# Spreading two gate rows over the partitions by DMA, and one value burst per group of the windowed attention

## The chip, the core and the metric

The kernel runs on one core of a Trainium2 chip. The metric is the device time of one execution in microseconds (us). The engines are TensorE (PE, whose weight loads are listed apart as PEld), VectorE (DVE), ScalarE (ACT), GpSimd (POOL) and SyncE (SP). SP issues nearly all DMAs; a few come from ACT's own queue. About 0.2% of the time (3.1 us) is what a measurement of this kernel can tell from no change.

## The reference

Two equal layers of a trunk are computed for five token tiles of 128 (four tiles of latent tokens, numbered 0 to 3, and one tile of context tokens, called LT). In each layer, cut to what matters here:

```python
def modulate_project(x, mod, w_in):
    shift, scale, gate = jnp.split(mod, 3, axis=-1)
    u = (layer_norm(x) * (1.0 + scale) + shift).astype(x.dtype)
    return split_columns(u @ w_in), gate

def attend_band(q, k, v, kc, vc, sink):      # branch C, |i - j| <= 128, plus 128 cached context keys
    ...
    p = softmax_with_sink(jnp.concatenate([s_band, s_ctx], axis=-1), sink).astype(v.dtype)
    o = (jnp.einsum('bkgnqs,bknsd->bkgnqd', p[..., :nband], vband)
         + jnp.einsum('bkgnqs,bksd->bkgnqd', p[..., nband:], vc))

def merge_residual(x, ys, zs, g_merge, gate, w_branch, w_out, ln_g, ln_b, alpha):
    gates = jnp.split(jax.nn.sigmoid(g_merge), N_BRANCH, axis=-1)
    merged = sum(gb * ((yb * jax.nn.silu(zb)) @ w_branch[i])
                 for i, (yb, zb, gb) in enumerate(zip(ys, zs, gates)))
    h = alpha * x + gate * (merged @ w_out)
    return (layer_norm(h) * ln_g + ln_b).astype(x.dtype)
```

`mod = silu(c) @ w_mod + b_mod`. Its last third, `gate`, is one row of 1024 numbers for the latent tokens and another for the context tokens. These two rows are the output gates of the title: every token of a tile is multiplied by the same row.

## The kernel before

Each layer is a list of weight pieces of 512 KB (two blocks of 128 rows by 512 columns). SP loads each piece into one of the three buffers of `raw`. For the projections GpSimd (in places ACT) splits it into a rounded part and a remainder in `wsp` or a slot, and TensorE multiplies with three products per block, 30 matmuls for a piece over five token tiles (L1057, by `product`). The order is written out by hand, engine by engine. PSUM has eight banks; `PsumPlan` says ahead which result uses which bank after which, and the engines wait for each other through `bank_full` and `bank_done`.

A layer runs branch A (attention), C (windowed attention) and B (mLSTM), in this order, and then the output projection. Branch C of layer 0 has a loop of 43 steps, of which the first 32 each handle one unit, that is one head for one latent tile. Step s does, on TensorE: the scores of unit s (L1252), the transposes of unit s - 3's probabilities (L1277), one part of a late modulation (`late_step`: L1001 products straight from a `raw` piece of `w_mod`, every fourth time the bias, L1008, and in a later step a transpose of the row, L1033) and then `values` for v = s - 8 (L1326). Four units are a group: two heads of one key head times two tiles. The value products of group g were made in two bursts: at v = 4g (part 0) those for the cached context keys and the first key block, at v = 4g + 2 (part 2) those for the other two blocks. Both read `pT`, the transposed probabilities of all four units, which part 0 waits for. The groups are eight; group g has its part 0 at step 4g + 8.

The late modulation of layer 0 needs 24 pieces of `w_mod`, used at steps 1, 4 and 7 to 28. A piece is not split; SP loads the piece three places on as soon as `mod_used` says that TensorE is through with the buffer. Chunk n of the modulation ends as one row per quarter of 128 columns, and DVE copies it to `mrow` (L2053). The last two chunks of a layer are the output gates. At that point the rows that matter are partitions 0, 32, 64 and 96 of `mrow` for the latent tokens and 1, 33, 65 and 97 for the context tokens, 128 numbers each, for both halves of `mrow`.

After the loop comes the merge projection G of branch C, half 0. It has four pieces, i = 0 to 3. Behind piece 2, `gates` (L1145) multiplied a column of the identity, repeated 128 times, with `mrow`: 16 fp32 matmuls per layer, which copy each row to all partitions of four PSUM banks. ACT copied the four banks to `gate_bc` (L1850), 128 partitions by 1024 for both kinds of tokens. ACT then takes the tanh of each G tile (L1938), and DVE uses the tanh and the branch product BR, whose banks are those of the G tiles (L2636). `gate_bc` is read at the end of the layer (L2661).

Of the kernel before, what the change touches and what calls it, by code (L numbers as in the profile page):

```python
# [18 lines left out]
F32 = mybir.dt.float32  # L19
# [225 lines left out]
def plan_layer(l, pieces, psum):  # L245
# [33 lines left out]
    for br in MERGE_ORDER:  # L279
# [78 lines left out]
        for hf in range(2):  # L358
            i = BRANCH[br]
            add((br, "G", hf), "in", KD, (COL_G + i * D + hf * HALF, HALF),  # L360
                part=(2, 3) if (br, hf) == ("C", 0) else None)
            add((br, "BR", hf), ("branch", i), BW // P, (hf * HALF, HALF))
            for name in ("G", "BR"):
                for t in range(T):
                    psum.roll((br, name, hf, t))
                if br != "B" and (name, hf) == ("G", 0):
                    keys = [(br, "PTctx", 0), (br, "PTctx", 1), (br, "Octx")]
                    for key in keys:
                        psum.roll(key)
                    if br == "C":  # L370
                        for i in range(4):
                            psum.take(("gate", i), psum.use[l, keys[i % 3]][0])
                if (br, name, hf) == ("B", "G", 0):
                    for c in range(T):
                        psum.take(("B", "yT", c), 1 + c % 3)
# [17 lines left out]
def trunk_kernel(nc, x_prompt, x_sample, cache_attn_k, cache_attn_v, cache_win_k, cache_win_v,  # L393
# [8 lines left out]
    with ctx:  # L402
# [194 lines left out]
        rdn_ready = each("rdn_ready")  # L597
        pick_ready = each("pick_ready")
        t4_used = each("t4_used")
# [378 lines left out]
        def _(pe):  # L978
# [10 lines left out]
            for l in range(DEPTH):  # L989
# [146 lines left out]

                def gates():

                    for i in range(4):
                        acquire(("gate", i))  # L1140
                        which, hf = i // 2, i % 2
                        wait_done(pe, ("gmod", len(LATE_CHUNKS[l]) - 2 + hf))
                        for q in range(4):
                            r = 32 * q + which
                            mm = pe.matmul(pb[:, bank_of(("gate", i)), tile_cols(q)], ident[:, r:r + 1].to_broadcast([P, P]),  # L1145
                                           mrow[:, hf, :], start=True, stop=True)
                        mm.then_inc(*full(("gate", i)))

                def late_step(s):
# [20 lines left out]
                def attention(br):  # L1170
# [124 lines left out]
                    def values(v):  # L1295
# [10 lines left out]
                        if br == "A":  # L1306
                            parts = ((T, 0, 1), (), (2, 3), ())[part]
                        else:
                            parts = ((T, 0), (), (1, 2), ())[part]
                        for i in parts:  # L1310
# [10 lines left out]
                            for e in range(2):  # L1321
# [6 lines left out]
                                               .rearrange("p u q -> p (u q)"),  # L1328
                                               start=(b == T), stop=(part == 2 and i == parts[-1]))
                        if part == 2:  # L1330
                            mm.then_inc(*(full(key) if hh else (pv_group[l], 1)))
# [14 lines left out]
                    def context(i, t):  # L1346


                        if (i, t) == (0, T - 1):
                            probs_context()  # L1350
                        if (i, t) == (1, T - 1):
                            values_context()
                        if br == "C" and (i, t) == (2, T - 1):
                            gates()

# [5 lines left out]
                def mlstm():  # L1361
# [63 lines left out]
                    def query_decay(m):  # L1425

                        key = ("B", "W", m)
                        acquire(key)
                        if m == 0:
                            pe.wait_ge(rx_ready[l], 2)  # L1430
                            pe.wait_ge(pick_ready[l], 1)
                        pe.matmul(bank(key), pick[0:GR2, m, :], R1X[0:GR2, :], start=True, stop=True)\
                            .then_inc(*full(key))
# [159 lines left out]
        def _(act):  # L1593
# [15 lines left out]
            for l in range(DEPTH):  # L1609
# [59 lines left out]
                def attention(br):  # L1669
# [176 lines left out]
                    if br == "C":  # L1846
                        act.wait_ge(stored[l], 64)
                        for i in range(4):
                            wait_full(act, ("gate", i))
                            act.copy(gate_bc[:, i // 2, (i % 2) * HALF:(i % 2 + 1) * HALF], bank(("gate", i)))\  # L1850
                                .then_inc(*done(("gate", i)))

# [160 lines left out]
        def _(dve):  # L2013
# [20 lines left out]
            for l in range(DEPTH):  # L2034
# [201 lines left out]
                def attention(br):  # L2236
# [128 lines left out]
                    def late_step(s):  # L2365

                        chunks = LATE_CHUNKS[l]
                        if s - 1 in MOD_AT[l][3::4]:
# [3 lines left out]
                            elif l:  # L2372
                                wait_full(dve, ("gate", 3), l - 1)
                            take_row(("gmod", n), n)
# [25 lines left out]
                def mlstm():  # L2400
# [14 lines left out]
                    ins.then_inc(gw_ready[l], 1)  # L2415
                    wait_full(dve, ("gate", 3))
                    dve.memset(v1[:, :, :, DV:DV + 1], 1.0)
# [74 lines left out]
                    for n in range(8):  # L2492
# [8 lines left out]
                    dve.tensor_copy(pick[:, :, :].rearrange("p m (b q) -> p (m b) q", b=2),  # L2501
                                    own[:, :].bitcast(F32).unsqueeze(2).to_broadcast([P, 2 * MH, HD])).then_inc(pick_ready[l], 1)

# [147 lines left out]
                dve.wait_ge(late_in[l], 16 * (T + 2))  # L2651
                for i in range(4):
                    wait_done(dve, ("gate", i))
                gated_at = {}
# [217 lines left out]
```

## Time and profile before

| | us |
|---|---|
| median of 3 runs | 1549.59 (1549.05 to 1552.27) |
| the profiled execution | 1550.15 |
| its span, first to last instruction | 1548.4 |
| TensorE busy in it | 1514.7 |
| VectorE, ScalarE, GpSimd busy | 731.7, 464.4, 643.7 |
| granted TensorE clock, mean, as a share of full speed | 0.999 |
| layer 0's branch C from its first value burst to the end of its last | 348.95 to 404.27 |
| `gates` on TensorE, layer 0 and layer 1 | 426.98 to 430.47, 1177.04 to 1180.53 |

The numbers of a timeline are a start and a duration in us from the start of the span, the engine, the line, what was written from what, and a count of records. An fp32 matmul leaves two records. Starts of successive TensorE rows say how long a stretch took; the durations overlap, since matmuls are pipelined.

### The profile page before, as it was taken

To read this page: it belongs to the slowest core of one execution; us is meant where nothing else is said; L and a number is where in the kernel's file an instruction comes from. 1 tells how busy PE (TensorE), PEld (TensorE's weight loads), DVE (VectorE), ACT (ScalarE), POOL (GpSimd) and SP (SyncE) were. 2 spreads that over 40 slices of the span, in tenths; PEclk is the share of its full clock that TensorE was granted. 3 is DMA by queue.
4 is the path that set the end of the run, shared out by engine and by line. 5 is a ranking of instruction groups with operands and counts; after the bars stand their busy time and mean duration, and the time that the engine had idled before them with its cause. 6 is when DMAs were issued, how large, how long until landed. Compare 5 with 4: busy or idle time off the path is not lost.

```text
span 1548.4 us, 22424 instructions
## 1 busy us (share of the span) xinstructions
PE 1514.7 (98%) x8995; PEld 1248.4 (81%) x8995; DVE 731.7 (47%) x1403; ACT 464.4 (30%) x1035; POOL 643.7 (42%) x573
## 2 busy tenths in 40 slices
PE   8999999999999999999999999999999999999997
PEld 6798788886788887788878977889768888778886
DVE  5596700656423333622497584126571136262257
ACT  1246710155410123411144485012661003242010
POOL 3561045720245453155773400556204554423562
PEclk9999999999999999999999999999999999999999
DMA  9421012327222222025431100223301221211421
GB/s 338 117 72 28 1 56 81 100 68 242 81 71 71 69 68 63 27 80 179 123 126 41 52 21 15 68 82 85 111 27 56 81 82 55 69 48 50 168 82 69
DMA packets 80487, 128.71 MB, mean 83 GB/s; under 512 B 16444, under 2 KB 29184, under 8 KB 80384
## 3 DMA queue, kind: packets, MB, share of 16 engines
q1 hardware_dynamic: 78144, 122.03, 25.8%
q10 hardware_dynamic: 2240, 5.24, 0.9%
q8 instruction: 72, 1.18, 0.3%
q14 instruction: 31, 0.25, 0.1%
HBM read 120.96 MB, written 6.30 MB: 82 GB/s over the span
## 4 chain that ended last, share of the span: by engine, by line
PE 83%; DVE 8%; POOL 4%; issue 2%; ACT 2%; DMA 1%; POOLq 0%; DVEq 0%; ACTq 0%; SPq 0%
PE pb L1057 56%; PE pb L1202 5%; PE pb L1326 4%; PE pb L1277 3%; PE pb L1082 3%; PE pb L1245 2%; PE pb L1001 2%; PE pb L1252 1%; PE pb L1507 1%; PE pb L1370 1%; DVE ks L2173 1%; DMA raw<-in_w_mod 1%; POOL slot_T L883 1%; POOL wsp L883 1%; DVE xh L2684 0%
## 5 line engine op out<-in xcount | busy, mean ns | idle before, releaser
L1057 PE MATMUL pb<-wsp,act_T 128*128 128x512 f32 x3048 | 713.2, 391 | 3.9 <-DVE act_T L2112 1.8
L1057 PEld LDWEIGHTS pb<-wsp,act_T 128*128 128x128 f32 x3048 | 568.0, 188 | 128.3 <-issue 7.1
L880 POOL CAST wsp<-raw 128x1024 fp32r<-128x1024 f32 x128 | 136.6, 1067 | 677.4 <-PE pb L1057 588.7
L883 POOL TENSOR_TENSOR wsp<-raw,wsp 128x512 fp32r<-128x512 f32 x268 | 360.3, 1365 | 10.2
L1057 PE MATMUL pb<-wsp,yT 128*128 128x512 f32 x720 | 165.7, 389 | 0.0
L1057 PEld LDWEIGHTS pb<-wsp,yT 128*128 128x128 f32 x720 | 135.0, 188 | 27.9
L2636 DVE SCALAR_TENSOR_TENSOR mt<-tg,pb 128x512 f32<-128x512 f32 x40 | 27.4, 685 | 216.6 <-PE pb L1057 215.8
L1938 ACT ACTIVATE tg<-pb 128x512 f32<-128x512 f32 x60 | 35.9, 599 | 275.9 <-PE pb L1057 275.9
L1277 PE MATMUL pb<-ident,pr 128*128 128x128 f32 x480 | 73.4, 274 | 3.0 <-ACT pT L1819 1.9
L2335 DVE TENSOR_SCALAR pr<-pr,rden 128x640 f32<-128x640 f32 (+2 forms) x128 | 69.1, 540 | 4.5
L2636 DVE SCALAR_TENSOR_TENSOR merged<-tg,pb 128x512 f32<-128x512 f32 x20 | 13.7, 687 | 119.9 <-PE pb L1057 119.9
L1277 PEld LDWEIGHTS pb<-ident,pr 128*128 128x128 f32 x480 | 57.2, 140 | 12.7 <-issue 4.7
L1202 PE MATMUL pb<-act_T,slot_T 128*128 128x320 f32 x384 | 61.0, 312 | 1.6 <-DVE zT L2245 1.6
L1202 PE MATMUL pb<-act_T,wsp 128*128 128x320 f32 x384 | 62.3, 314 | 0.1
L2314 DVE TENSOR_REDUCE nm<-pb 128x1 f32<-128x640 f32 x64 | 52.3, 820 | 14.1 <-PE pb L1245 14.1
L1202 PEld LDWEIGHTS pb<-act_T,slot_T 128*128 128x128 f32 x384 | 56.8, 188 | 2.5 <-DVE zT L2245 2.1
L1202 PEld LDWEIGHTS pb<-act_T,wsp 128*128 128x128 f32 x384 | 56.6, 188 | 0.4 <-POOL wsp L883 0.4
L1245 PE MATMUL pb<-kT,qT 128*128 128x320 f32 x256 | 53.5, 332 | 2.7 <-ACT pr L1784 2.5
L1775 ACT ACTIVATE pr<-pr,nm 128x385 f32<-128x385 f32 (+1 forms) x64 | 43.1, 673 | 34.2 <-DVE nm L2321 33.8
L1784 ACT ACTIVATE pr<-pb,nm 128x640 f32<-128x640 f32 x64 | 51.9, 811 | 2.5 <-DVE nm L2314 2.4
L2321 DVE CUSTOM_DVE_ANT_0 pr<-pb,edges,sink 128x384 f32<-128x384 f32 (+1 forms) x64 | 43.4, 680 | 19.5 <-PE pb L1252 18.9
L1245 PEld LDWEIGHTS pb<-kT,qT 128*128 128x128 f32 x256 | 37.8, 188 | 14.7 <-issue 9.2
(303 smaller groups left out, 1963.7 us busy)
## 6 DMA issues: line engine op xcount, KB each, us to landing
raw<-in_w_in SPq DMA_DIRECT2D x112, 512.0 KB, 3.6
raw<-in_w_mod SPq DMA_DIRECT2D x32, 512.0 KB, 4.6
raw<-in_w_branch SPq DMA_DIRECT2D x24, 512.0 KB, 3.6
raw<-in_w_out SPq DMA_DIRECT2D x16, 512.0 KB, 3.6
stage<-in_w_mod SPq DMA_DIRECT2D x28, 256.0 KB, 7.3
raw<-in_w_in SPq DMA_DIRECT2D x16, 256.0 KB, 5.0
xh<-in_x_sample SPq DMA_DIRECT2D x6, 512.0 KB, 6.5
out<-xh ACTq DMA_DIRECT2D x5, 512.0 KB, 3.0
```

The source lines that it names most:

```text
L880: pool.tensor_copy(hi, raw[:, p % 3, :, 0:width]).then_inc(raw_hi, 1)
L883: ins = pool.tensor_tensor(lo[:, j, :], raw[:, p % 3, j, 0:width], hi[:, j, :].bitcast(F32), ALU.subtract)
L1057: mm = pe.matmul(dst, lhs(a, k, t), w[:, wa, j, 0:width], start=(k == 0 and n == 0), stop=(i == count - 1 and j == 1 and n == 2))
L1082: mm = pe.transpose(pb[:, b, tile_cols(i % 4)], src(i), ident[:, :])
L1202: mm = pe.matmul(pb[:, b + h, 0:320], w[:, wa, j, tile_cols(c)], act_T[:, a, k, h * 320:(h + 1) * 320], start=(k == 0 and m == 0), stop=(k ...
L1245: mm = pe.matmul(pb[:, b + i, 0:320], q, kT[:, kv, a, i * 320:(i + 1) * 320], start=(a == 0), stop=(a == 1))
L1277: mm = pe.transpose(pb[:, bank_of((br, "PT", s)), tile_cols(i)], probs(br, s)[:, tile_cols(i)], ident[:, :])
L1326: mm = pe.matmul(pb[r, bank_of(key), (2 * hh + lo) * P:(2 * hh + hi) * P], v_of, pT[:, g % 2, place_of, 2 * e + lo:2 * e + hi, :] .rearran ...
L1784: act.activation(probs(br, s).rearrange("p (a n) -> p a n", a=2), pb[:, b:b + 2, 0:320], ACT.Exp, bias=nm[:, o], accum_out=lsum[:, o]).the ...
L2314: dve.tensor_reduce(nm[:, o], pb[:, b:b + 2, 0:320], AX.XY, ALU.max, negate=True)\
L2321: dve.tensor_tensor_reduce(out=probs(br, s)[:, 0:n], in0=pb[:, b, 0:n], in1=edge_row(t), scale=-1.0, scalar=sink[:, 1, h:h + 1], op0=ALU.a ...
L2335: dve.tensor_scalar(p, p, rden[:, o], None, ALU.mult).then_inc(p_ready[l], 1)
```

## The change

Three things change.

- `gates` is gone from TensorE, with its four turns on PSUM banks. In its place ACT issues 16 DMAs per layer, once it has waited for DVE's copies to `mrow`. Each takes 128 numbers (512 bytes) of one partition of `mrow` and writes them to all 128 partitions of `gate_bc` (64 KB). All add 16 to one semaphore, `gate_in`.
- Who waits for the gates waits for `gate_in`: the copy to `mrow` in layer 1 (L2053) and the first use of `gate_bc` (L2661). A wait of DVE before a memset at the start of the mLSTM is gone. To have a semaphore for `gate_in`, `pick_ready` is one for both layers.
- In branch C of layer 0 all value products of a group are made at part 0. Layer 1 and branch A keep their two bursts.

```diff
-                def gates():
-
-                    for i in range(4):
-                        acquire(("gate", i))
-                        which, hf = i // 2, i % 2
-                        wait_done(pe, ("gmod", len(LATE_CHUNKS[l]) - 2 + hf))
-                        for q in range(4):
-                            r = 32 * q + which
-                            mm = pe.matmul(pb[:, bank_of(("gate", i)), tile_cols(q)], ident[:, r:r + 1].to_broadcast([P, P]),
-                                           mrow[:, hf, :], start=True, stop=True)
-                        mm.then_inc(*full(("gate", i)))
...
                         if br == "A":
-                            parts = ((T, 0, 1), (), (2, 3), ())[part]
+                            parts, last = ((T, 0, 1), (), (2, 3), ())[part], (2, 3)
+                        elif l == 0:
+                            parts, last = ((T, 0, 1, 2), (), (), ())[part], (0, 2)
                         else:
-                            parts = ((T, 0), (), (1, 2), ())[part]
+                            parts, last = ((T, 0), (), (1, 2), ())[part], (2, 2)
...
-                        if part == 2:
+                        if part == last[0]:
                             mm.then_inc(*(full(key) if hh else (pv_group[l], 1)))
...
                     if br == "C":
                         act.wait_ge(stored[l], 64)
-                        for i in range(4):
-                            wait_full(act, ("gate", i))
-                            act.copy(gate_bc[:, i // 2, (i % 2) * HALF:(i % 2 + 1) * HALF], bank(("gate", i)))\
-                                .then_inc(*done(("gate", i)))
+                        for hf in range(2):
+                            wait_done(act, ("gmod", len(LATE_CHUNKS[l]) - 2 + hf))
+                            for r in (32 * q + which for which in range(2) for q in range(4)):
+                                at = hf * HALF + r // 32 * P
+                                act.dma_start(gate_bc[:, r % 32, at:at + P],
+                                              mrow[r:r + 1, hf, :].unsqueeze(1).to_broadcast([1, P, P])).then_inc(gate_in, 16)
...
                             elif l:
-                                wait_full(dve, ("gate", 3), l - 1)
+                                dve.wait_ge(gate_in, 16 * 16 * l)
...
-                    wait_full(dve, ("gate", 3))
                     dve.memset(v1[:, :, :, DV:DV + 1], 1.0)
...
                 dve.wait_ge(late_in[l], 16 * (T + 2))
-                for i in range(4):
-                    wait_done(dve, ("gate", i))
+                dve.wait_ge(gate_in, 16 * 16 * (l + 1))
```

TensorE in the middle of layer 0's branch C, before, from the bias of a chunk on; the two rows of `cached` and `kv` are part 0 of a group whose part 2 follows behind the transpose of `mrow`:

```order
L1008 MATMUL pb<-bmod,ident 32x128 x4
L1326 MATMUL pb<-pT,cached 64x256 x2
L1326 MATMUL pb<-pT,kv_54 64x128 x2
L1252 MATMUL pb<-kT,qT 128x384 x2
L1277 MATMUL pb<-ident,pr 128x128 x3
L1001 MATMUL pb<-raw,csil 32x128 x8
L1252 MATMUL pb<-kT,qT 128x512 x2
L1277 MATMUL pb<-ident,pr_145 128x128 x4
L1001 MATMUL pb<-raw,csil 32x128 x8
L1033 MATMUL pb<-ident,mrow 128x128
L1326 MATMUL pb<-pT,kv_54 64x256 x4
L1252 MATMUL pb<-kT,qT 128x384 x2
```

The same place in the changed program:

```order
L1006 MATMUL pb<-bmod,ident 32x128 x4
L1314 MATMUL pb<-pT,cached 64x256 x2
L1314 MATMUL pb<-pT,kv_54 64x128 x2
L1314 MATMUL pb<-pT,kv_54 64x256 x4
L1238 MATMUL pb<-kT,qT 128x384 x2
L1263 MATMUL pb<-ident,pr 128x128 x3
L999 MATMUL pb<-raw,csil 32x128 x8
L1238 MATMUL pb<-kT,qT 128x512 x2
L1263 MATMUL pb<-ident,pr_145 128x128 x4
L999 MATMUL pb<-raw,csil 32x128 x8
L1031 MATMUL pb<-ident,mrow 128x128
L1238 MATMUL pb<-kT,qT 128x384 x2
```

The four matmuls of part 2 stand two steps earlier, right behind part 0; the number of matmuls is the same.

TensorE at the end of the same loop, before, from the transposes of unit 29 on; the first two rows of L1326 are part 0 of group 6, the next two its part 2, the last three group 7, and L1057 is the merge projection:

```order
L1277 MATMUL pb<-ident,pr 128x128 x3
L1326 MATMUL pb<-pT,cached 64x256 x2
L1326 MATMUL pb<-pT,kv_54 64x256 x2
L1277 MATMUL pb<-ident,pr 128x128 x4
L1277 MATMUL pb<-ident,pr_145 128x128 x3
L1326 MATMUL pb<-pT,kv_54 64x256 x2
L1326 MATMUL pb<-pT,kv_54 64x128 x2
L1326 MATMUL pb<-pT,cached 64x256 x2
L1326 MATMUL pb<-pT,kv_54 64x128 x2
L1326 MATMUL pb<-pT,kv_54 64x256 x4
L1057 MATMUL pb<-wsp,act_T 128x512 x30
```

And in the changed program:

```order
L1263 MATMUL pb<-ident,pr 128x128 x3
L1314 MATMUL pb<-pT,cached 64x256 x2
L1314 MATMUL pb<-pT,kv_54 64x256 x4
L1314 MATMUL pb<-pT,kv_54 64x128 x2
L1263 MATMUL pb<-ident,pr 128x128 x4
L1263 MATMUL pb<-ident,pr_145 128x128 x3
L1314 MATMUL pb<-pT,cached 64x256 x2
L1314 MATMUL pb<-pT,kv_54 64x128 x2
L1314 MATMUL pb<-pT,kv_54 64x256 x4
L1055 MATMUL pb<-wsp,act_T 128x512 x30
```

Part 2 of group 6 no longer stands between the last transposes and group 7.

ACT from the last cast of branch C's `yT` on, before, with what each row waits for:

```order
L1844 CAST yT<-ytmp 128x4x128 [waits bank_done0]
L1850 COPY gate_bc<-pb 128x512 [waits bank_full6,stored0]
L1850 COPY gate_bc<-pb 128x512 [waits bank_full7]
L1850 COPY gate_bc<-pb 128x512 [waits bank_full0]
L1850 COPY gate_bc<-pb 128x512 [waits bank_full6]
L1938 ACTIVATE tg<-pb 128x512 [waits y_ready0,bank_full1]
```

And in the changed program:

```order
L1830 CAST yT<-ytmp 128x4x128 [waits bank_done0]
L1838 DMA gate_bc<-mrow 128x1x128 [waits bank_done6,stored0]
L1838 DMA gate_bc<-mrow 128x1x128 x7
L1838 DMA gate_bc<-mrow 128x1x128 [waits bank_done7]
L1838 DMA gate_bc<-mrow 128x1x128 x7
L1926 ACTIVATE tg<-pb 128x512 [waits y_ready0,bank_full1]
```

Sixteen DMA issues stand where four copies stood, and the tanh of the first G tile is queued behind them.

## Rows read from the trace of the kernel before

**Rows 1.** The page's first part: busy us of each engine, share, instructions.
```profile
PE 1514.7 (98%) x8995; PEld 1248.4 (81%) x8995; DVE 731.7 (47%) x1403; ACT 464.4 (30%) x1035; POOL 643.7 (42%) x573
```

**Rows 2.** Timeline of TensorE around `gates`, layer 0.
```profile
426.98 3.73 PE L1145 MATMUL pb<-mrow,ident 128*128 128x128 f32 x32
430.47 7.08 PE L1057 MATMUL pb<-wsp,act_T 128*128 128x512 f32 x30
437.39 4.92 PE L1057 MATMUL pb<-wsp,yT 128*128 128x512 f32 x21
```

**Rows 3.** The same in layer 1.
```profile
1177.04 3.73 PE L1145 MATMUL pb<-mrow,ident 128*128 128x128 f32 x32
1180.53 7.08 PE L1057 MATMUL pb<-wsp,act_T 128*128 128x512 f32 x30
```

**Rows 4.** Timeline of ACT around the gate copies, layer 0, then layer 1.
```profile
420.89 0.62 ACT L1844 CAST yT<-ytmp 128x512 fp32r<-128x512 f32 x1 [7.95 <-DVE ytmp L2341]
...
428.13 0.58 ACT L1850 COPY gate_bc<-pb 128x512 f32<-128x512 f32 x1 [6.61 <-PE pb L1145]
...
432.14 0.60 ACT L1938 ACTIVATE tg<-pb 128x512 f32<-128x512 f32 x1 [0.81 <-PE pb L1057]
...
1178.18 0.58 ACT L1850 COPY gate_bc<-pb 128x512 f32<-128x512 f32 x1 [6.61 <-PE pb L1145]
```

**Rows 5.** Timeline of SP's queue: issues of DMAs, start, us, count.
```profile
3.97 2.02 SPq L727 DMA_DIRECT2D stage<-in_w_mod  x4
...
8.32 8.74 SPq L727 DMA_DIRECT2D stage<-in_w_mod  x8
...
751.28 0.47 SPq L765 DMA_DIRECT2D cached<-in_cache_attn_v  x1
```

**Rows 6.** DMA view of 421.5 to 437 us, then GpSimd's timeline.
```profile
raw<-in_w_in SPq DMA_DIRECT2D x2, 512.0 KB, 3.5
...
444.49 1.04 POOL L880 CAST wsp<-raw 128x1024 fp32r<-128x1024 f32 x1 [3.13 <-PE pb L1057]
```

**Rows 7.** Tile view of `gate_bc`: count, ns min/median/max, first to last start.
```profile
L2661 DVE TENSOR_TENSOR ot<-pb,gate_bc x19: 672/680/696, 749.1 to 1537.6; 128x512 f32<-128x512 f32 x19
```

**Rows 8.** Windows view: stretch, busy us (x) by engine, clock, DMA share, GB/s.
```profile
348.95:404.27 55.32, 54.41 (x649) 36.38 (x645) 35.23 (x114) 32.33 (x90) 4.05 (x22) 1.00 0.67 209
```

**Rows 9.** Timeline of TensorE, steps 12 to 16 of layer 0's branch C.
```profile
357.72 0.65 PE L1326 MATMUL pb<-pT,cached 128*64 128x256 f32 x4
...
358.52 0.62 PE L1252 MATMUL pb<-kT,qT 128*128 128x384 f32 x2
...
359.40 0.64 PE L1001 MATMUL pb<-raw,csil 128*32 128x128 f32 x16
...
361.90 1.08 PE L1326 MATMUL pb<-pT,kv 128*64 128x256 f32 x8
362.92 0.62 PE L1252 MATMUL pb<-kT,qT 128*128 128x384 f32 x2
...
365.35 0.64 PE L1001 MATMUL pb<-raw,csil 128*32 128x128 f32 x16
```

**Rows 10.** Timeline of TensorE at that loop's end, then of ACT.
```profile
400.38 0.98 PE L1277 MATMUL pb<-ident,pr 128*128 128x128 f32 x7
401.30 0.87 PE L1326 MATMUL pb<-pT,kv 128*64 128x256 f32 x8
402.61 0.65 PE L1326 MATMUL pb<-pT,cached 128*64 128x256 f32 x4 [0.44 <-ACT pT L1819]
...
404.27 7.12 PE L1057 MATMUL pb<-wsp,act_T 128*128 128x512 f32 x30
...
402.08 0.48 ACT L1819 COPY pT<-pb 128x384 f32<-128x384 f32 x1
```

**Rows 11.** DMA view of 335 to 400 us, then TensorE's wait.
```profile
raw<-in_w_mod SPq DMA_DIRECT2D x23, 512.0 KB, 4.7
...
383.24 0.65 PE L1001 MATMUL pb<-raw,csil 128*32 128x128 f32 x16 [0.47 <-DMA raw<-in_w_mod]
```

More of the change, by code:

```diff
@@ L369, in plan_layer @@
                         psum.roll(key)
-                    if br == "C":
-                        for i in range(4):
-                            psum.take(("gate", i), psum.use[l, keys[i % 3]][0])
                 if (br, name, hf) == ("B", "G", 0):
@@ L597, in trunk_kernel @@
         rdn_ready = each("rdn_ready")
-        pick_ready = each("pick_ready")
+        pick_ready = sem("pick_ready")
+        gate_in = sem("gate_in")
         t4_used = each("t4_used")
@@ L1328, in values @@
                                                .rearrange("p u q -> p (u q)"),
-                                               start=(b == T), stop=(part == 2 and i == parts[-1]))
-                        if part == 2:
+                                               start=(b == T), stop=((part, i) == last))
+                        if part == last[0]:
                             mm.then_inc(*(full(key) if hh else (pv_group[l], 1)))
@@ L1352, in context @@
                             values_context()
-                        if br == "C" and (i, t) == (2, T - 1):
-                            gates()
                     return context
@@ L1430, in query_decay @@
                             pe.wait_ge(rx_ready[l], 2)
-                            pe.wait_ge(pick_ready[l], 1)
+                            pe.wait_ge(pick_ready, l + 1)
                         pe.matmul(bank(key), pick[0:GR2, m, :], R1X[0:GR2, :], start=True, stop=True)\
@@ L2501, in mlstm @@
                     dve.tensor_copy(pick[:, :, :].rearrange("p m (b q) -> p (m b) q", b=2),
-                                    own[:, :].bitcast(F32).unsqueeze(2).to_broadcast([P, 2 * MH, HD])).then_inc(pick_ready[l], 1)
+                                    own[:, :].bitcast(F32).unsqueeze(2).to_broadcast([P, 2 * MH, HD])).then_inc(pick_ready, 1)
                     def query_decay(m):
@@ L2651, in _ @@
                 dve.wait_ge(late_in[l], 16 * (T + 2))
-                for i in range(4):
-                    wait_done(dve, ("gate", i))
+                dve.wait_ge(gate_in, 16 * 16 * (l + 1))
                 gated_at = {}
```

## The prediction

> **What bounds the kernel now.** I read the page first, for the busy times. TensorE is busy for 1514.7 us of a span of 1548.4, and no other engine for half of it [rows 1]. So whatever takes TensorE's time counts in full wherever nothing else is late, and I ask of each stretch that the change touches whether TensorE waits in it. The timeline of TensorE around `gates` shows none: the products of L1145 start at 426.98, the next piece at 430.47, the first branch product at 437.39, each right behind the one before [rows 2]. The windows view of layer 0's branch C, from its first value burst to its end, has 54.41 us busy out of 55.32 [rows 8]. There, too, TensorE sets the pace, but with company: the DMA share is 0.67, and the two waits of the stretch are for a piece of `w_mod` (0.47 us, [rows 11]) and for ACT at the end (0.44 us, [rows 10]). The timelines of ACT and of SP's queue then say what the new DMA issues meet.
>
> **Part 1, the gate products go.** In layer 0 TensorE spends 430.47 - 426.98 = 3.49 us on them [rows 2], in layer 1 1180.53 - 1177.04 = 3.49 us [rows 3]. GpSimd is ahead: the pieces that follow start without a wait, and GpSimd's own next cast, at 444.49, waits for TensorE, not the reverse [rows 6]. Nothing is late next, so the term is 2 x 3.49 = **-6.98 us**.
>
> **Part 2, sixteen DMA issues on ACT.** ACT ends its cast at 420.89 + 0.62 = 421.51 and then idles for 6.61 us until the first gate bank is full; layer 1 has the same 6.61 [rows 4]. No row has a copy from one partition of SBUF to all. The nearest rows for an issue are those of SP: 0.47 us for 64 KB in a quiet queue, and four of 256 KB in 2.02 us, 0.5 each with the gaps between them [rows 5]. At 0.5 us the sixteen take 8 us. ACT would be free at 429.5. The first tanh stands behind them. It started at 432.14 [rows 4], and without the gate products it could start at 428.65; so it comes 0.9 us late. Who waits for it? DVE, and TensorE when the first branch product takes the bank of the first G tile, at 437.39 - 3.49 = 433.90 [rows 2]. The tanh takes 0.60 us, so the bank is free at 430.1 with 3.8 us to spare, and the later tiles come every 1.4 us while ACT needs 0.6. I cost the issues at **0**, under this cover; it is gone when one issue takes more than (433.90 - 0.60 - 421.51) / 16 = 0.74 us. From the other side, ACT's four copies (4 x 0.58 us) disappear, which gains nothing, since it waited.
>
> The data have time. `gate_bc` is first read at 749.1 [rows 7], over 300 us later, and `mrow` is overwritten in layer 1 much later still; the new waits on `gate_in` find it full. The copies share the DMA engines with the weights. A weight piece issued in that stretch lands in 3.5 us [rows 6], and is issued about two pieces before its turn, 2 x (437.39 - 430.47) = 13.8 us [rows 2]; it may take 10 us longer than it does. The sixteen copies of 64 KB are 1 MB, two pieces more. Cost 0. The removed wait of DVE before a memset and the shared `pick_ready` move nothing on the path.
>
> **Part 3, one value burst per group.** The work is the same, and what can be saved is what a burst costs to begin. Part 0 of a group takes 358.52 - 357.72 = 0.80 us for eight records and part 2 362.92 - 361.90 = 1.02 us for eight, together 1.82 [rows 9]. Group 7 already runs as one burst, since its steps have nothing between them: 404.27 - 402.61 = 1.66 us for its sixteen [rows 10]. So joining saves 0.16 us per group. It holds for groups 0 to 6, 7 x 0.16 = **-1.1 us**; group 7 gains nothing. TensorE's page in the Trainium skill (TensorE: Matmul & The Clock Gate, Back-to-back issue gap) gives a warm 256-column matmul 256/2.4 + 2.5 ns = 109 ns whatever stands before it, 0.87 us for eight, and knows no cost of beginning; by it this term is zero. The row has 1.02 for eight and 1.66 for sixteen.
>
> Against this stand two costs. **The end of the loop.** Before, part 2 of group 6 ran between the last transposes and group 7. From the start of the last transposes to the start of group 7 it is 402.61 - 400.38 = 2.23 us, and ACT ends it: its last copy of `pT` runs from 402.08 to 402.56 [rows 10]. Part 2 of group 6 began at 401.30 inside this, and its 0.8 us cost only cover. After the change it stands before the transposes, and ACT's 2.23 us behind them are as long as before: TensorE will stand still for 0.44 + 0.8 us. This costs **+0.8 us**.
>
> **The pieces of `w_mod`.** From step 7 to 28 each step consumes one, and SP loads the piece three steps ahead when one is used up. From the end of step 13's products (359.40 + 0.64 = 360.04) to the start of step 16's (365.35) there are 5.31 us, of which part 2 at step 14 took 1.02 [rows 9]. After the change those three steps have no values at all: 4.29 us remain, against a median landing of 4.7 us [rows 11] and 0.1 us before the issue. So the piece of every step that is a multiple of 4 is late by about 0.5 us if its landing stays at the median. There are five such steps (12, 16, 20, 24, 28): at most 5 x 0.5 = 2.5 us. From below, the shorter landing of 3.5 us [rows 6], seen where pieces are issued far apart, makes it zero; and the 0.47 us wait of today [rows 11] could even go, since three of four pieces get more time. The issue that decides comes after the long step, with a burst of 1.66 us between it and the one before, and so has the DMA engines more to itself than the median one. I take **+1.0 us**, between the ends and nearer the median's.
>
> Sum: -6.98 - 1.1 + 0.8 + 1.0 = **-6.3 us**. The profiled execution took 1550.15 us, 1.75 more than its span; less 6.3 it is 1543.85. It lay 0.56 us above the median of the runs, so I predict a median of 1543.85 - 0.56 = **1543.3 us**, -0.4%.
>
> **The rivals.**
>
> *ACT gets stuck in its issues (slower).* One mechanism, in one place: the sixteen copies back up in ACT's queue and ACT, which issues in order with its tanh, stands. SP's rows show that this happens: four issues of 256 KB at 3.97 take 2.02 us, 0.5 each, and once the queue is full, from 8.32 on, eight take 8.74, 1.09 each [rows 5]. If each of ACT's took 1.09 us, ACT would be free at 421.51 + 17.4 = 438.9, and the bank of the first G tile at 439.5 in place of 433.90: a stall of 5.6 us in each layer. The time would be 1543.3 + 11.3 = 1554.6. It decides from 0.74 us per issue; the gain of 3.1 us per layer is eaten up at 421.51 + 16 p + 0.60 = 433.90 + 3.1, p = 0.93 us. For it: all rows come from one partition at a time, which no row of this trace shows, and two thousand packets in 8 us are many. Against it: those eight of SP's bring 256 KB each in 1.09 us, so it was their data that filled the DMA engines, which a copy of 64 KB does in a quarter of the time; and ACT's queue is empty when the first comes. The Trainium skill (SBUF — State Buffer, Door 1: The DMA port swizzle) says that the bandwidth of a DMA depends on how many of the 16 ports its partitions reach, 436 GB/s for all; by it a source in one partition has 27 GB/s, 64 KB take 2.4 us, and the sixteen 38 us. That is this rival's condition; how much of the 38 us ACT would stand depends on how many copies its queue holds, and no row here shows such a copy or that number. Chance 0.10.
>
> *The bursts cost more than they save.* Beginning a burst costs nothing that joining saves, and all five late pieces are late by the 0.5 us. Then the sum is -6.98 + 0.8 + 2.5 = -3.7, and the time 1545.9. For it: the landing times of the stretch, which are already above those elsewhere. Against it: group 7's 1.66 us. Chance 0.15.
>
> *The bursts save and nothing is late.* The pieces land in under 4.2 us: -6.98 - 1.1 + 0.8 = -7.3, 1542.3; with today's 0.47 us wait gone, 1541.8. Chance 0.15.
>
> *Nothing changes*, because a later engine gives the 3.49 us back in each layer. For this something would have to be late in 430 to 437 us or in what follows. TensorE is the one that everything waits for there. Chance 0.03.
>
> **How the numbers follow.** The forecast, 1542.5 to 1545, has 0.57. The range takes in the two cases of the bursts: **1541.3 to 1546.2**; what is left out is the stuck ACT, the case of no change, and some of the edges, about 0.16. A measurement of this kernel can tell some 0.2%, 3.1 us, from no change. Faster than 1546.5: 0.57 + 0.15 + 0.15 = 0.87, less a little for the dearer burst case, 0.86. Within 0.2%: 0.06. Slower than 1552.7: 0.08, nearly all the stuck ACT.
>
> **What would show it.** In the profile after: no L1145 rows, and the last G piece right behind the third in both layers. ACT's sixteen issues between about 421 and 429.5 us, less some; a pitch over 0.74 us and a wait of the branch product for ACT's tanh would be the first rival. In layer 0's branch C eight bursts of 1.66 us; PE waits for `raw` at the products of steps 12, 16, 20, 24 and 28, 1.0 us in all over what there was; and a wait of about 1.2 us for ACT's `pT` before group 7. The prediction is wrong if ACT's issues take longer than an issue from SP does, or if the waits for `w_mod` sum up to more than 2.5 us.

## The result and the profile after

The changed kernel takes 1572.32 us (median of 4 runs) beside 1549.32 for the kernel before on the same chip: 1.0146 times as long, 95% interval 1.0129 to 1.0164. The forecast was 1543.3. The profiled execution has a span of 1569.9 us, 21.5 more than before.

The timeline of TensorE in the changed kernel, around the place where `gates` was, first in layer 0 and then in layer 1, shows where the time went (the last row of each is cut off where the window ends):

```profile
418.52 13.89 PE L1055 MATMUL pb<-wsp,act_T 128*128 128x512 f32 x60
445.19 16.24 PE L1055 MATMUL pb<-wsp,yT 128*128 128x512 f32 x60 [12.78 <-ACT tg L1926]
461.27 18.98 PE L1055 MATMUL pb<-wsp,act_T 128*128 128x512 f32 x83
...
1180.30 13.89 PE L1055 MATMUL pb<-wsp,act_T 128*128 128x512 f32 x60
1206.68 16.06 PE L1055 MATMUL pb<-wsp,yT 128*128 128x512 f32 x60 [12.48 <-ACT tg L1926]
1222.57 22.60 PE L1055 MATMUL pb<-wsp,act_T 128*128 128x512 f32 x99
```

The last two G pieces run as one row of 60 records, so the products of `gates` are gone as intended. But the first branch product, which came right behind them before [rows 2], now waits 12.78 and 12.48 us for ACT's tanh. ACT's own timeline in layer 0 says why, and the tile view of `gate_bc` gives all 32 copies of both layers (count, ns min/median/max of one issue, first and last start; then us from issue to landing):

```profile
419.36 0.62 ACT L1830 CAST yT<-ytmp 128x512 fp32r<-128x512 f32 x1 [7.95 <-DVE ytmp L2329]
419.42 24.93 ACTq L1838 DMA_DIRECT2D gate_bc<-mrow  x16
444.45 2.56 ACT L1926 ACTIVATE tg<-pb 128x512 f32<-128x512 f32 x5 [24.47 <-issue]
...
L1838 ACTq DMA_DIRECT2D gate_bc<-mrow x32: 488/1450/2928, 419.4 to 1203.3; - x32
...
DMA to landing us min/median/max: 4.5/6.3/8.6
```

The sixteen issues take 24.93 us, 1.56 each, where [rows 5] had 0.5. All five tanh then run at once.

There is a second loss behind the wait. The windows view (stretch, busy us and count of PE, PEld, DVE, ACT, POOL, then granted clock, DMA share, GB/s) of the wait and of the 60 records behind it:

```profile
432.35:445.19 12.84, 0.06 (x2) 0.03 (x1) 0.00 (x0) 0.74 (x2) 3.52 (x3) 0.66 0.74 116
445.19:461.27 16.08, 16.08 (x61) 13.12 (x61) 5.04 (x7) 1.81 (x4) 4.03 (x3) 0.84 0.21 24
```

In the wait, with TensorE idle, the granted clock falls, and in the stretch behind it its mean is 0.84 of 2.4 GHz, so part of it ran at 1.2 GHz. The same 60 records took 13.60 us in the kernel before: they start at 437.39 [rows 2], and the row behind them, in that kernel's timeline, is

```profile
450.99 27.36 PE L1057 MATMUL pb<-wsp,act_T 128*128 128x512 f32 x120
```

So layer 0 loses 12.78 us by the wait and 16.08 - 13.60 = 2.48 us by the clock, layer 1 12.48 and 15.89 - 13.60 = 2.29; together 30.0. The products of `gates` give 6.98 back. That leaves 23.0 to lose, of which 21.5 are seen. The rest, 1.5 us, lies before the G projection of layer 0's branch C, which starts at 402.72 in place of 404.27 [rows 10]. Half of it, 0.78 us, is the loop with its bursts; the other 0.77 was gained before the first value burst (348.17 in place of 348.95), where nothing was changed, and is a difference between two executions: in the variants of the changed kernel that burst starts anywhere from 348.17 to 350.61.

### The profile page after: what moved, and what is told of

It is laid out like the page before. It is cut to its first block, busy times and chain, and to the rows that moved or that the text cites. A ratio compares the mean times of both kernels' runs of the same rounds, so it can differ in the third digit from the quotient of the medians.

```text
span 1569.9 us, 22308 instructions
## 1 busy us (share of the span) xinstructions
PE 1510.5 (96%) x8931; PEld 1243.8 (79%) x8931; DVE 731.2 (47%) x1403; ACT 458.7 (29%) x1027; POOL 643.8 (41%) x573
## 4 chain that ended last, share of the span: by engine, by line
PE 79%; DVE 8%; ACTq 3%; POOL 3%; issue 2%; ACT 2%; DMA 1%; SPq 1%; POOLq 0%; DVEq 0%
PE pb L1055 53%; PE pb L1188 5%; PE pb L1314 4%; ACTq L1838 3%; PE pb L1263 3%; PE pb L1080 3%; PE pb L1231 2%; PE pb L999 1%; PE pb L1238 1%; PE pb L1493 1%; PE pb L1356 1%; DVE ks L2161 1%; POOL slot_T L881 1%; DMA stage<-in_w_mod 1%; DVE pr L2323 1%
## 5 line engine op out<-in xcount | busy, mean ns | idle before, releaser
L1055 PE MATMUL pb<-wsp,yT 128*128 128x512 f32 x720 | 170.5, 397 | 25.3 <-ACT tg L1926 25.3
L1055 PEld LDWEIGHTS pb<-wsp,yT 128*128 128x128 f32 x720 | 138.3, 193 | 55.0 <-issue 26.0
```

The costliest lines, as they stand in the source:

```text
L1055: mm = pe.matmul(dst, lhs(a, k, t), w[:, wa, j, 0:width], start=(k == 0 and n == 0), stop=(i == count - 1 and j == 1 and n == 2))
```

## The experiments

The theory after the result: **A**, ACT stands in its issues, its tanh and with it a PSUM bank are late, and nothing else costs. Two questions are below it: why one issue takes 1.56 us (**P**: because all rows come out of one SBUF partition; **D**: because rows of 512 bytes are slow from anywhere; **F**: because of the form of the access pattern), and what the bursts do.

**One part of the change at a time.** First the copies without the bursts.

```diff
-                        elif l == 0:
-                            parts, last = ((T, 0, 1, 2), (), (), ())[part], (0, 2)
```

> The change without its value bursts (layer 0's branch C keeps two bursts per group); gates by DMA as in the change. Theory A (the copies alone make it slower: ACT stands in its sixteen issues for about 25 us, TensorE waits 12.5 to 12.8 us per layer and then runs about 2.4 us longer at the lower clock, less 2 x 3.49 for the products): 1573, since the bursts save about 1 us. Rival B (the bursts share in the loss): 1560 or less. Theory A expects 16 issues of about 1.5 us and the same two waits.

Measured: 1574.08 us, ratio 1.0152 (1.0138 to 1.0165); sixteen issues in 24.78 us and two waits for the tanh, 24.0 us together. Without the bursts the loss is 24.1 us over the kernel before (1550.01), so the copies make all of it.

Then the bursts without the copies:

> The kernel before with the value bursts of the change alone. By the trace of the changed kernel, whose loop of layer 0's branch C was 0.8 us shorter from its first burst on: 1548.3 to 1548.9, about -0.8 us. By the terms of the prediction (entry saved 1.1, cover lost 0.8, late pieces 1.0): +0.7, 1550.0.

Measured: 1549.27 beside 1550.01, ratio 0.9997 (0.9988 to 1.0006), which decides nothing about 0.7 us. The traces do, below.

**The copies moved behind the tanh.** The same sixteen issues, taken out of their old place and put in 15 us later in ACT's order (the added lines):

```diff
                            act.activation(tg[:, t, :], bank((br, "G", hf, t)), ACT.Tanh, scale=0.5)\
                                .then_inc(*done((br, "G", hf, t)))
+                        if (br, hf) == ("C", 0):
+                            act.wait_ge(stored[l], 64)
+                            for h2 in range(2):
+                                wait_done(act, ("gmod", len(LATE_CHUNKS[l]) - 2 + h2))
+                                for r in (32 * q + which for which in range(2) for q in range(4)):
+                                    at = h2 * HALF + r // 32 * P
+                                    act.dma_start(gate_bc[:, r % 32, at:at + P],
+                                                  mrow[r:r + 1, h2, :].unsqueeze(1).to_broadcast([1, P, P])).then_inc(gate_in, 16)
```

> The change with the sixteen issues of each layer moved behind the five tanh of branch C's first G half. Nothing else differs. Theory A (only that the tanh and so a PSUM bank stand behind the issues costs time): ACT still stands about 25 us, from 433 to 458, but its next tanh is due only at about 467; no wait of TensorE for ACT's tg, and 1549.3 - 7.0 - 0.8 = 1541.5. Rival C (the copies slow the weights or something else too): above 1545.

Measured: 1541.66 us, ratio 0.9943 (0.9930 to 0.9957), the fastest of the variants that fill `gate_bc` with the gates. ACT's timeline (last tanh of the half, then the issues) and TensorE's:

```profile
434.69 0.60 ACT L1918 ACTIVATE tg<-pb 128x512 f32<-128x512 f32 x1 [0.76 <-PE pb L1055]
434.75 24.76 ACTq L1926 DMA_DIRECT2D gate_bc<-mrow  x16
...
420.76 13.89 PE L1055 MATMUL pb<-wsp,act_T 128*128 128x512 f32 x60
434.49 13.76 PE L1055 MATMUL pb<-wsp,yT 128*128 128x512 f32 x60
448.09 27.36 PE L1055 MATMUL pb<-wsp,act_T 128*128 128x512 f32 x120
```

ACT still stands 24.76 us, and no row of TensorE waits. The weight pieces issued between 415 and 465 us landed in 5.2 us, not 3.5, and nobody noticed. The windows view of the 60 records that run beside the copies has them in the 13.60 us of the kernel before, at the full clock, with a DMA share of 0.66:

```profile
434.49:448.09 13.60, 13.60 (x61) 11.26 (x60) 5.03 (x7) 0.60 (x1) 7.62 (x6) 1.00 0.66 85
```

Theory A holds from this side: the same copies with the same slowness cost nothing where no one waits behind them.

**ACT late without any DMA.** To that version, 22 copies of 128x512 before the first tanh of the half:

```diff
+                            if (br, hf, t) == ("C", 0, 0):
+                                for _ in range(22):
+                                    step(act.copy(tg[:, t, :], zT[:, 0, 0:HALF]))
```

> The copies behind the tanh, and ACT kept busy before its first tanh of that half by 22 copies of 128x512 that nobody needs, each waiting for the one before (about 0.75 us each, 16.5 us, from 429 to 445 us). No DMA stands before the tanh. Theory A (the loss is ACT's lateness and the lower clock behind it, nothing of the DMA traffic): TensorE waits about 13 us per layer and its next 60 matmuls take 2.4 us longer, 1541.7 + 2 x 15.4 = 1572. If the copies' traffic had its own share in the change's loss, this run is faster than that by as much.

Measured: 1566.66 us, ratio 1.0103 (1.0087 to 1.0118). One copy took 0.65 us, not 0.75, so the waits were shorter than planned:

```profile
428.31 14.28 ACT L1920 COPY tg<-zT 128x512 f32<-128x512 f32 x22 [7.03 <-PE pb L1055]
...
443.36 16.47 PE L1055 MATMUL pb<-wsp,yT 128*128 128x512 f32 x60 [9.65 <-ACT tg L1921]
459.67 20.56 PE L1055 MATMUL pb<-wsp,act_T 128*128 128x512 f32 x90
```

By its own trace it should lose 2 x 9.65 us of waits and, for the 60 records behind them, 16.31 - 13.60 and 15.50 - 13.60, in all 23.9; its span is 1565.6 against 1541.7, 23.9 more. That the two agree to a tenth is luck, since by the medians it is 25.0 (1566.66 against 1541.66); what they leave for anything else is about 1 us. So lateness and clock are the price, and no DMA has to stand before the tanh for it. Both versions have the copies' traffic behind the tanh, so this run does not measure the traffic; the 13.60 us above do.

**What makes an issue slow.** Five variants of the change differ in what the copies read. In all five `gate_bc` does not hold the gates in their places, and each was timed once; what is read from them is the length of the issues, which differs by more than ten microseconds. First all 128 partitions as the source:

```diff
-                                              mrow[r:r + 1, hf, :].unsqueeze(1).to_broadcast([1, P, P])).then_inc(gate_in, 16)
+                                              mrow[:, hf, :]).then_inc(gate_in, 16)
```

> The change with another source of the sixteen copies: all 128 partitions of mrow, 512 bytes each, to the same places (so gate_bc does not hold the gates). Same count of copies, of rows of 512 bytes and of bytes. Theory P (one source partition is what is slow): the issues fall to about 0.5 us each, ACT is free before its tanh is due, no wait, a span of about 1541. Theory D (rows of 512 bytes are slow wherever they come from, 0.11 us each on 16 engines): as the change, 25 us of issues and a span near 1570.

Then 16 partitions, 8 times each (`mrow[0:16, hf, :].unsqueeze(1).to_broadcast([16, 8, P])`):

> The change with each of the sixteen copies reading 16 partitions of mrow, each 8 times over, in place of one partition 128 times (so gate_bc does not hold the gates). Same rows, bytes and issues. Theory P: the data come out of more partitions at once, so the issues fall towards the 0.65 us of the 128-partition source and the wait of TensorE goes, 1541; if the partitions share a way out by groups, a time between. If only a source of all 128 is fast: as the change, 1572.

Then HBM (`b_mod[0:1, r // 32 * P:(r // 32 + 1) * P].to_broadcast([P, P])`), and the same in the form of the change (`.unsqueeze(1).to_broadcast([1, P, P])`):

> The change with the sixteen copies reading 512 bytes of b_mod in HBM, repeated to 128 partitions, in place of a partition of mrow (so gate_bc does not hold the gates). Theory P (one SBUF partition as the source is slow): fast, issues of about 0.5 us, no wait, span about 1541. Theory D (512-byte rows are slow): as the change. A third (any source address read 128 times over is slow, also in HBM): as the change too, but then the run with 128 source partitions is fast.

> The change with the source in HBM, the access pattern kept in the change's form (1 x 128 x 128, the repeat in the second place; the earlier HBM run had 128 x 128). Theory P (the single SBUF partition): fast, 0.45 us per issue, 1542. Rival F (the form of the pattern makes the descriptors slow, wherever the data are): as the change, 1.5 us per issue, 1572.

And last, one partition again, but rows of 1 KB in half as many copies (`mrow[r:r + 1, :, :]`, 256 numbers, to `gate_bc[:, r % 32, at:at + 2 * P]`):

> The change with eight copies per layer of 1 KB rows (both halves of a partition of mrow, to neighbouring places of gate_bc, so the order of the gates there is another): the same bytes out of one partition at a time in half as many rows and half as many issues. Theory P by bytes (about 37 GB/s out of a partition): the data take as long, 28 us, and ACT stands for most of it, 20 us or more. Theory D by rows: half the time, 13 us of issues, TensorE waits about 1 us per layer.

ACT's timelines, in the order 128 partitions, 16 partitions, HBM, HBM in the change's form, 1 KB rows:

```profile
419.45 10.73 ACTq L1838 DMA_DIRECT2D gate_bc<-mrow  x16
```

```profile
421.42 13.02 ACTq L1838 DMA_DIRECT2D gate_bc<-mrow  x16
```

```profile
420.86 8.68 ACTq L1838 DMA_DIRECT2D gate_bc<-in_b_mod  x16
```

```profile
421.05 11.69 ACTq L1838 DMA_DIRECT2D gate_bc<-in_b_mod  x16
```

```profile
420.89 25.46 ACTq L1838 DMA_DIRECT2D gate_bc<-mrow  x8
```

| source of the copies | issues, us | landing, median us | time, us, one run |
|---|---|---|---|
| one partition (the change) | 24.9 for 16 | 6.3 | 1572.3 (median of 4) |
| one partition, 1 KB rows | 25.5 for 8 | - | 1574.65 |
| 16 partitions | 13.0 | 3.6 | 1544.74 |
| 128 partitions | 10.7 | 2.4 | 1541.39 |
| HBM, 1 x 128 x 128 | 11.7 | 3.5 | 1543.05 |
| HBM, 128 x 128 | 8.7 | 3.4 | 1542.94 |

P holds and D falls: 512-byte rows are fast as soon as they come from HBM or from 16 partitions. (Sixteen partitions leave one wait of 0.9 us for the tanh, in layer 0.) The 1 KB rows confirm it from the other side: half the rows and half the issues, but the same bytes out of one partition and the same 25 us. F is a small effect, 3.0 us of sixteen issues, 0.19 each. The DMA view of ACT's queue (packets, MB) puts a rate on it, in the changed kernel from 424 to 444 us and with 1 KB rows from 426 to 446:

```profile
q10 hardware_dynamic: 1729, 0.79, 53.7%
```

```profile
q10 hardware_dynamic: 786, 0.71, 65.5%
```

That is 0.79 MB and 0.71 MB in 20 us, 40 and 36 GB/s. From 16 partitions the same queue moves 0.78 MB in 10 us (424 to 434), 78 GB/s. About four of the slow copies are on their way at any time (a landing of 6.3 us over a distance of 1.56), and ACT ends an issue only as an earlier copy drains. Four is no fixed number of places: with HBM as the source, 128 x 128, it is six (3.4 us over 0.54), with a median of 0.45 us for an issue. What sets the limit was not tested. Nor do the runs tell one partition from one address read over and over: that a repeated address is not slow as such is shown for HBM, and for SBUF only up to the 8 repeats of the run with 16 partitions.

**Eight before, eight after.** In the change, the copies of the first half stay and those of the second go behind the tanh.

> The change with the eight copies of the first half where they were and the eight of the second half behind the five tanh of the first G half. If ACT stands 1.56 us for each, it is free at 419.4 + 12.5 = 432, its tanh done at 432.6, and TensorE needs the bank at 432.4: a wait of 0 to 0.7 us per layer, 1541.5 to 1543. If the first issues are cheap because the queue is empty (0.6, 1.3, 0.6, 1.5 us in the change), no wait and 1541.5.

Measured: 1544.09 us, ratio 0.9959 (0.9945 to 0.9974).

```profile
420.55 12.46 ACTq L1838 DMA_DIRECT2D gate_bc<-mrow  x8
...
433.11 0.60 ACT L1926 ACTIVATE tg<-pb 128x512 f32<-128x512 f32 x1 [12.00 <-issue]
...
433.85 13.88 PE L1055 MATMUL pb<-wsp,yT 128*128 128x512 f32 x60 [0.31 <-ACT tg L1926]
```

Eight issues take 12.46 us, half of sixteen, and TensorE waits 0.31 us (0.32 in layer 1): ACT had room for about eight of these copies in this place. The time is above the expected 1541.5 to 1543 and 2.4 us above that of the sixteen behind the tanh, of which the two waits are 0.6; the intervals of the two overlap, and the profiled spans differ by 0.2 (1541.9 and 1541.7), so nothing is built on the difference.

**The issues on SP.** Before the first weight piece of the second G half, with SP waiting for what ACT's order gave for free:

```diff
+                    if p == pieces.first[l, ("C", "G", 1)]:
+                        wait_full(sp, ("C", "Octx"))
+                        sp.wait_ge(stored[l], 64)
+                        for hf in range(2):
+                            wait_done(sp, ("gmod", len(LATE_CHUNKS[l]) - 2 + hf))
...
+                                sp.dma_start(gate_bc[:, r % 32, at:at + P],
```

> The change with the sixteen issues on SP's queue, right before the first weight piece of branch C's second G half. Theory A': SP stands as long as ACT did, 25 us, and the pieces queued behind it come late: the first is issued at 446 in place of 421, about when GpSimd wants it (439), so TensorE waits some 10 us per layer, 1560. If SP's queue issues without standing (0.5 us each): 1541.5. In either case ACT's tanh is on time.

Measured: 1561.44 us, ratio 1.0075 (1.0058 to 1.0091).

```profile
420.32 24.43 SPq L828 DMA_DIRECT2D gate_bc<-mrow  x16
444.80 10.73 SPq L745 DMA_DIRECT2D raw<-in_w_in  x4
...
455.19 24.99 PE L1064 MATMUL pb<-wsp,act_T 128*128 128x512 f32 x101 [7.48 <-POOL wsp L890]
```

SP stands as long as ACT did, so the slowness belongs to the copy and not to the queue. Here the weight piece behind it is late, and TensorE waits for GpSimd (15.6 us in four waits, the two of every kernel at the start of some 1 us among them).

**The bursts.** First the row of the kernel before at which step 12's products start, then the rows of the changed kernel that answer [rows 9] and [rows 10], TensorE from step 12 to step 16 and at the end of the loop:

```profile
356.80 0.64 PE L1001 MATMUL pb<-raw,csil 128*32 128x128 f32 x16
```

```profile
355.68 0.65 PE L999 MATMUL pb<-raw,csil 128*32 128x128 f32 x16
356.25 0.42 PE L1006 MATMUL pb<-bmod,ident 56*32 56x128 f32 x8
356.60 0.65 PE L1314 MATMUL pb<-pT,cached 128*64 128x256 f32 x4
357.09 1.25 PE L1314 MATMUL pb<-pT,kv 128*64 128x128 f32 x12
358.27 0.62 PE L1238 MATMUL pb<-kT,qT 128*128 128x384 f32 x2
...
363.89 0.64 PE L999 MATMUL pb<-raw,csil 128*32 128x128 f32 x16
...
394.52 0.63 PE L1263 MATMUL pb<-ident,pr 128*128 128x128 f32 x4 [0.34 <-ACT pT L1805]
...
401.06 0.65 PE L1314 MATMUL pb<-pT,cached 128*64 128x256 f32 x4 [1.24 <-ACT pT L1805]
```

A joined burst takes 358.27 - 356.60 = 1.67 us. From step 12's products to step 16's it is 8.21 us; before, those of step 12 started at 356.80 and those of step 16 at 365.35 [rows 9], 8.55. So this group saves 0.34 us: 0.15 inside the burst, 1.82 - 1.67, and 0.19 elsewhere. Most of that lies where part 2 stood: the transpose of `mrow` starts 0.25 us before part 2 in the kernel before (361.65 to 361.90) and 0.09 us before the scores that follow it now (361.39 to 361.48). From one group's burst to the next, less the waits for `w_mod`, groups 0 to 3 save 0.34 to 0.37 us each and group 4 saves 0.15; group 5 loses 0.17 and group 6 0.65. For at the end the wait for ACT's `pT` is 1.24 in place of 0.44, and a new one of 0.34 stands before the last transposes. From the first burst to the end of the last, less the waits for `w_mod`, the loop takes 54.85, 54.86 and 54.78 us in the three traces without joined bursts (before, the copies alone, the copies behind the tanh without bursts) and 54.13 in three with them (the change, the bursts alone, the copies behind the tanh): the bursts save **0.7 us**.

The last run asked whether that reaches the total, with the copies behind the tanh and no bursts:

> The copies behind the tanh, as in the run with the sixteen issues moved, but without the value bursts. Against the 1541.7 of that run: 1542.5 if the bursts save 0.8 us also here, 1541.7 or less if they save nothing.

Measured: 1543.28 us, ratio 0.9953 (0.9940 to 0.9965), beside 0.9943 (0.9930 to 0.9957) with the bursts. The order is the expected one, but the intervals overlap; the 0.7 us rest on the traces. This run also prices the gate products alone: 1550.43 - 1543.28 = 7.15 us, beside the 6.98 of their term.

## Why the prediction was wrong, point by point

**Part 1, the gate products, -6.98 us: right.** With the copies out of the way and no joined bursts the total is 7.15 us lower; with the bursts it is 8.35 (1550.01 to 1541.66), of which this term is 6.98 and the bursts 0.7, and the rest is within what the runs scatter.

**Part 2, the sixteen issues, cost 0: this is the step that failed.** It put the issues at 0, under a cover of 0.74 us each, and that cost is what failed; the rest of its chain held. ACT was free at the expected place (the first issue even starts at 419.42, 0.06 us after the start of the cast and not at its end, which makes the cover 0.6 us longer in all), the first tanh stood behind the issues, TensorE needed the bank at 437.39 less 3.49 less what the bursts gave, and the cover was nearly as long as worked out; the run with eight copies before the tanh shows the edge, 12.46 us with a wait of 0.31. What was wrong is 0.5 us for one issue. It came from the rows of SP, whose copies read HBM [rows 5]; the copies of the change read one partition of SBUF and take 1.56, so that ACT is late by 12.78 and 12.48 us for TensorE where the sum had nothing. The same 64 KB from HBM do take 0.54 to 0.73 each, so the row was right for what it showed and was used for something that it did not show. The prediction's own sign, ACT's issues taking longer than one from SP, is there.

**The first rival was the truth, and it too was undersized.** The text had its mechanism, its place and its point of decision, and it had what the Trainium skill says (SBUF — State Buffer, Door 1: The DMA port swizzle), that the bandwidth of a DMA goes by how many of the 16 ports its partitions reach, some 27 GB/s for one port; an estimate from that is 38 us for the sixteen. The trace agrees in kind and not in the figure: it has 36 to 40 GB/s, and the measurement decides. The prediction wrote the 38 us down and then let ACT's queue hold an unknown number of copies, and gave 0.10. If the data take 38 us and the issuer may be ahead by only a few copies, the issuer stands for nearly all of it. About four copies are ahead here, and with that the estimate for the issues would have been twelve drained copies of 2.4 us, 29 us, against 24.9 measured. It is also where the argument that ACT's queue is empty when the first comes went wrong: an empty queue helps only the first few. In the run with ACT busy, where the issues begin between the tanh, the first three take 0.6 us each and the other thirteen 21.32, 1.64 each.

**The rival's price, 1554.6, was short by 18 us** for two reasons: 1.56 us per issue in place of 1.09 (7.5 us per layer), and the clock, which the sum did not have at all (2.48 and 2.29 us). That is 19.8 us; the bursts, 1.4 us better than forecast, and the earlier first issue, 0.6 per layer, give some of it back. The waits of 9.65 to 12.78 us seen here were each followed by a stretch partly at the lower clock.

**Part 3, entries saved, -1.1: undersized.** Each of groups 0 to 3 saves 0.34 us or a little more in place of 0.16, because leaving a burst out also frees the change of work before it, which group 7, from which the 0.16 was read, cannot show. The Trainium skill (TensorE: Matmul & The Clock Gate, Back-to-back issue gap) gives the gap of an isolated matmul by its columns alone, with no term for a beginning; these rows do not agree with a sum made that way, since the same sixteen records take 1.82 us in two bursts and 1.67 in one.

**The end of the loop, +0.8: right for the wait that it named.** 1.24 - 0.44 = 0.80 us; the other 0.34 before the last transposes was not seen coming.

**The pieces of `w_mod`, +1.0: wrong.** The waits from the first burst on are 0.42, 0.27 and 0.26 us in the same three traces with joined bursts and 0.47, 0.21 and 0 without. Three steps without values last no 4.29 us but less, yet the piece that decides lands in time, as the text held possible and then did not believe enough. The value bursts as a whole were put at +0.7 us and are -0.7.

## What to carry to other kernels

The price of a DMA on a compute engine's queue is not the issue alone: with slow copies the engine was only about four ahead of the data here, so what is queued behind the issues waits for the bytes to move. Ask of every copy how many partitions it reads, and place the issues where the engine has nothing due for as long as the data take; here a move behind five tanh turned +1.5% into -0.6%. And when a rare case has a rule that gives it a duration, put that duration into the sum rather than into a tenth of a chance.

## What the runs showed of the hardware

- Copies out of one SBUF partition move at 40 GB/s in rows of 512 bytes and at 36 in rows of 1 KB, while their packets take 54% and 66% of the time of the 16 DMA engines. From 16 partitions the queue moves 78 GB/s and the sixteen issues take 13.0 us, from all 128 10.7, against 24.9. Whether it is the partition or a port that it shares with others was not separated: successive copies read partitions 0, 32, 64 and 96.
- About four such copies of 64 KB are on their way at a time, on ACT's queue as on SP's (landing 6.3 and 6.4 us over 1.56 and 1.53), and the issuing engine stands. From HBM it is six, at a median of 0.45 us for an issue, so four is not a number of places that holds for every copy.
- With HBM as the source, the form 1 x 128 x 128 costs 0.73 us per issue and 128 x 128 0.54.
- Waits of TensorE of 9.7 to 12.8 us for ACT cost 1.9 to 2.7 us more in the 60 records behind them, at a mean clock of 0.84 in the one stretch read.
- The same 60 records beside the copies' traffic, at a DMA share of 0.66 and with no wait before them, take the 13.60 us that they take without it.
